# A fused transformer block in one launch: attention transposes within the projections, and two expert tiles ahead of the weight stage

## The chip, the cores and the metric

One core of a Trainium2 chip runs the whole program in one launch. The metric is the time of one execution on the device in microseconds, the median of several; lower is better. Engines in this text: TensorE (PE) multiplies and transposes, VectorE (DVE), ScalarE (ACT) and GpSimd (POOL) work on elements, SyncE (SP) issues the loads and stores.

## The reference, cut to what matters

The input has 256 tokens of width 1024. Two residual layers with a per-layer gated addition come first, then a mixing layer, a cross attention on a memory and a layer of many small experts.

```python
# first attention layer (16 heads of 64), called moba
q, k, v, z = split(rms_norm(x) @ w_in)
q, k = rope(rms_norm(q) * q_gain), rope(rms_norm(k) * k_gain)
x = x + (softmax(q k^T / 8, causal) v * silu(z)) @ w_out
x = x + sigmoid(rms_norm(x) @ w_gate) * (p @ w_proj)
# second layer (nsa): three branches per head (compressed, selected, window), each a
# masked softmax attention, added with learned gates, * silu(z), @ w_out; then the same gated addition
# mixing layer: a linear recurrence beside a chunked attention, @ w_out
# cross attention: 4 heads of 256 on 256 memory rows
x = x + (softmax(q_mem k_mem^T / 16) v_mem) @ w_o_mem
# experts (peer): 8 heads pick 16 of 128*128 experts for each token by two top-16 lists
sc = (h @ w_query) . sub_keys ; top 16 of the sums ; g = softmax(top)
x = x + sum over the picked e of g_e * gelu(h . u_e) * v_e
out = rms_norm(x)
```

## The kernel before

**Projections.** All weight matrices run as one stream of chunks of 512 columns, each in two halves ("units", 1 MB). SP loads a unit into one of four slots. ACT copies it rounded to `whi` (`split`, L1169), POOL writes the rest, weight minus `whi`, into `wlo` (L1093), and PE adds three products, `hThi*whi`, `hThi*wlo`, `hTlo*whi` (`project`, L721), each a pass of 16 matrix products in a half chunk. `whi` and `wlo` hold two units: `split` of a unit waits until PE is done with the unit two before. `take(c)` on ACT (L1188, L1199) first splits two later units and then copies chunk c out of PSUM. For the first layer, chunks 0 to 3 hold q and k, 4 and 5 v, 6 and 7 the gate z. DVE rotates q and k (`rope_chunk`), PE transposes them with the identity (`transposes`, L619) in groups of four blocks into two PSUM banks in turn (a group waits until the one two before is copied), and DVE copies each group out (`take_transposed`, L1573 to L1578). All eight groups of the first layer run between the last projection and the attention.

**Attention.** `attention(phase)` is written out by hand on PE, DVE and ACT as one loop over jobs (a head and a block of 128 queries): PE makes the score of job i (L820), DVE the mask and the maximum (L1744), ACT the exponential (L1270), PE transposes P of job i-3 (L827), ACT copies it out (L1261), PE multiplies by V for job i-4 (L838), DVE scales the result. Scores go to banks 6, 7 and 1 in turn, so they run three jobs ahead; chunks of a projection use banks 0 and 1 or 2 and 3. Phase 0 has 32 jobs, phase 1 96, phase 3 (memory) 8. In phases 0 and 1 `last_gates` puts the tanh of the gate between ACT's jobs (L1246, L1249), and DVE turns it into gate factors. Finished parts of the output are transposed as "pieces" (`piece`, L628), split into `hThi` and `hTlo` by DVE or ACT (L1648, L1207, L1658), and the output projection begins on them (`unit_of_pieces`, L650).

**Experts.** One tile is 128 experts: `u` (1024 columns) and `v` (1024 columns). An activation tile is 24 products (L635, L638) of `u` with the tokens, an output tile 12 products of 512 columns (L1045) in two token halves. While DVE selects the experts, PE computes the activations of the last NA = 30 tiles ahead ("ahead" tiles); E_AT and SEL0_AT say behind which of them exp and the first selection transposes stand. The slots of these tiles end up with `u` and `v` of tiles 0 and 1 (`head`). Then 64 weight groups of four tokens follow: DVE makes one-hot rows (L2101), POOL multiplies the gate in (L1097), PE multiplies the two (L1025), ACT copies the gate weights to `arena` and `kept_w` (L1444, L1445), POOL weighs the ahead tiles (L1103). When these are done SP loads tiles 2, 3, 4, and the tile loop runs: activation of tile i, output of tile i-1; a load waits for the low part of `v` three tiles before. The loop does tiles 0 to 97, the tail the 30 ahead tiles' outputs.

The excerpt that a program prints below shows the functions that the change touches.

Of the kernel before, what the change touches and what calls it, by code (L numbers as in the profile page):

```python
# [8 lines left out]
ALU = mybir.AluOpType  # L9
# [4 lines left out]
P = 128  # L14
# [20 lines left out]
SEL0_AT = 19  # L35
SCALE = HD ** -0.5
# [55 lines left out]
def build(nc, x_d, mem_d, keep_d, tab_d, sml_d, frt_d, final_d, w_d, sk_d, ex_d, out_d):  # L92
    ctx = ExitStack()
    with ctx:
# [116 lines left out]
        half_done, half_out = sem("half_done"), sem("half_out")  # L211
        hot_ready, wt_done, wt_taken = sem("hot_ready"), sem("wt_done"), sem("wt_taken")
# [240 lines left out]
        def piece_of(name, u):  # L453

            src, gain = {"moba_o": (OR, None), "nsa_o": (OR, None), "ple0": (x, "ple_gain0"), "norm1": (x, "norm1"),
                         "ple1": (x, "ple_gain1"), "mem": (OR, "mem"), "cross": (OR, "cross"), "mem_o": (OR, None),
                         "ffn": (OR, "ffn")}[name]
            b = bank[{"moba_o": (0, 0, 0, 4), "nsa_o": (0, 0, 0, 4), "mem_o": (0, 1, 4, 5)}.get(name, (4, 5, 6, 7))[u]]
            return dict(src=src, bank=b, out=b[:, :].rearrange("p (b q) -> p b q", b=2), at=slice(2 * u, 2 * u + 2),
                        gain=None if gain is None else sm(gain)[:, 2 * u:2 * u + 2])  # L460
# [28 lines left out]
        def tr_all(name):  # L489
# [9 lines left out]
                enumerate(sorted(((q // 2, q % 2) for q in range(4)), key=lambda tp: (2 * tp[0] + tp[1] - NA) % 4))]  # L499

# [107 lines left out]
        def _(pe):  # L608
            mm = nc.tensor.matmul

            def transposes(name):
                groups, signals = tr_base(name)
                for i, g in enumerate(TR[NAMES.index(name)][1]):
# [177 lines left out]
            def gated_piece(phase, name, i):  # L791

                if phase == 3:
                    if i == LAST_JOB[3, 1] + 6:
                        pe.wait_ge(o_taken, PHASES[3][LAST_JOB[3, 1]]["number"] + 1)
                        piece(name, 0)
                        piece(name, 1)
                    return
                for u in range(3):
                    if i == piece_ends(phase, u) + 8:  # L800
                        if u > 0:
                            pe.wait_ge(piece_lo[u - 1], nth(name))
# [168 lines left out]
            for u in range(2):  # L971
                pe.wait_ge(piece_lo[u], nth("mem_o"))
# [43 lines left out]
            transposes("sel1")  # L1016
            pe.wait_ge(aa_gelu, NA)
# [116 lines left out]
        def _(act):  # L1134
# [190 lines left out]
            take(first_of("nsa_z") + 1, scale=x_scale)  # L1325
# [106 lines left out]
            for i in range(NA):  # L1432
# [42 lines left out]
            def finish_tile(i, ge, g):  # L1475

                ge(a_done, i + 1)
                ge(glo_ready, i - 1)
                gelu(i)
                ge(v_done, i - 1)  # L1480
# [3 lines left out]
                hi_g(i)  # L1484

            def iteration(i, ge, g):
                if g is not None or i >= 2:
                    loaded(i, ge)
                    ge(a_done, i - 1)
                    hi_u(i)  # L1490
                if i > 0:
                    finish_tile(i - 1, ge, g)
# [5 lines left out]

            expert_loop(act, iteration)
# [22 lines left out]
        def _(dve):  # L1522
# [614 lines left out]
            def iteration(i, ge, g):  # L2137
                if g is not None or i >= 2:
# [3 lines left out]
                if i > 0:  # L2142
# [163 lines left out]
```

## Time and profile before

| | |
|---|---|
| median of 3 runs | 1652.11 us (1650.27 to 1652.24) |
| profiled execution | 1652.1 us, of which span 1650.3 |
| mean granted clock of PE | 0.974 |
| PE busy | 1537.2 us (93%) |
| DVE, ACT, POOL busy | 896.4, 819.6, 567.0 us (54%, 50%, 34%) |
| DMA | 238.47 MB, 145 GB/s on average |

The time of an execution is the span, from the first instruction to the last, and a little around it. A granted clock of 1.00 is PE's upper level, 0.50 its lower. A busy share counts a whole execution; the timeline rows further down show single places.

### The profile page before, as it was taken

What the parts mean: (1) busy time and instruction counts of PE and PEld (TensorE: products, weight loads), DVE (VectorE), ACT (ScalarE), POOL (GpSimd) and SP (SyncE); (2) the same over time, 40 slices, a digit from 0 to 9 for tenths busy, and PEclk for the clock granted to TensorE, in tenths of its full rate; (3) what the DMA queues carried; (4) which work ended last, traced back from release to release, by engine and by line L of the source; (5) the groups of instructions that cost most, each with busy time, mean ns of one, the idle gap of its engine ahead of it and who ended that gap; (6) DMA issues with size and microseconds to landing.
All of it is one profiled execution on the core that took longest, in us unless ns stands there. A gap on an engine that the chain in (4) does not pass through costs nothing.

```text
span 1650.3 us, 28298 instructions
## 1 busy us (share of the span) xinstructions
PE 1537.2 (93%) x10643; PEld 1416.6 (86%) x10643; DVE 896.4 (54%) x2125; ACT 819.6 (50%) x1435; POOL 567.0 (34%) x256
## 2 busy tenths in 40 slices
PE   6998999989979979988999789999999999999998
PEld 5987899978869869978999668999999999999886
DVE  6826248478342332122796894555555555555565
ACT  4546444388434724434455564444444444444444
POOL 5770656510455546725588992000000000000000
PEclk9998999999989979999999999999999999999999
DMA  6750244510233234424254003545555555555453
GB/s 255 274 182 23 106 151 154 206 51 2 78 127 109 97 129 147 159 84 144 81 198 161 1 0 144 188 178 183 195 181 180 189 191 178 182 194 183 172 197 128
DMA packets 37529, 238.47 MB, mean 145 GB/s; under 512 B 4160, under 2 KB 4288, under 8 KB 13248
## 3 DMA queue, kind: packets, MB, share of 16 engines
q1 hardware_dynamic: 37440, 237.27, 40.0%
q8 instruction: 57, 0.93, 0.2%
q14 instruction: 32, 0.26, 0.1%
HBM read 236.21 MB, written 1.05 MB: 144 GB/s over the span
## 4 chain that ended last, share of the span: by engine, by line
PE 65%; POOL 6%; DVE 4%; issue 3%; ACT 3%; POOLq 0%; DVEq 0%; ACTq 0%
PE bank L1045 21%; PE bank L635 15%; PE bank L638 7%; PE bank L718 6%; PE bank L721 4%; POOL raw L1097 3%; PE bank L820 2%; PE bank L678 2%; PE bank L838 2%; POOL wlo L1093 2%; PE bank L650 1%; POOL arena L1103 1%; ACT whi L1169 1%; PE bank L628 1%; PE bank L827 1%
## 5 line engine op out<-in xcount | busy, mean ns | idle before, releaser
L1093 POOL TENSOR_TENSOR wlo<-raw,whi 128x2048 fp32r<-128x2048 f32 x42 | 194.2, 4626 | 204.0 <-ACT whi L1169 204.0
L1093 POOL TENSOR_TENSOR wlo<-arena,whi 128x2048 fp32r<-128x2048 f32 x42 | 193.6, 4615 | 178.2 <-ACT whi L1169 178.2
L635 PE MATMUL bank<-hThi,whi 128*128 128x256 f32 x1024 | 250.3, 282 | 1.2 <-ACT xw L1445 1.2
L635 PE MATMUL bank<-hTlo,whi 128*128 128x256 f32 x1024 | 250.0, 282 | 0.0
L1045 PE MATMUL bank<-whi,ghi 128*128 128x512 f32 x512 | 202.9, 396 | 0.3 <-DVE glo L2133 0.3
L1045 PE MATMUL bank<-whi,glo 128*128 128x512 f32 x512 | 202.9, 396 | 0.0
L1045 PE MATMUL bank<-wlo,ghi 128*128 128x512 f32 x512 | 202.1, 395 | 0.0
L635 PEld LDWEIGHTS bank<-hThi,whi 128*128 128x128 f32 x1024 | 194.7, 190 | 5.6 <-issue 1.6
L635 PEld LDWEIGHTS bank<-hTlo,whi 128*128 128x128 f32 x1024 | 195.0, 190 | 4.2 <-issue 0.2
L1462 ACT ACTIVATE gact<-bank 128x256 f32<-128x256 f32 x98 | 37.8, 386 | 266.6 <-PE bank L638 266.6
L2128 DVE TENSOR_TENSOR gact<-gact,arena 128x256 f32<-128x256 f32 x98 | 41.7, 426 | 201.2 <-ACT gact L1462 201.2
L1169 ACT ACTIVATE whi<-raw 128x2048 fp32r<-128x2048 f32 x42 | 80.5, 1916 | 129.6 <-PE bank L721 60.3
L638 PE MATMUL bank<-hThi,wlo 128*128 128x256 f32 x1024 | 143.7, 283 | 0.0
L1169 ACT ACTIVATE whi<-arena 128x2048 fp32r<-128x2048 f32 x42 | 80.4, 1914 | 120.6 <-PE bank L721 70.3
L638 PEld LDWEIGHTS bank<-hThi,wlo 128*128 128x128 f32 x1024 | 132.1, 192 | 0.0
L2123 DVE TENSOR_TENSOR wlo<-raw,whi 128x1024 fp32r<-128x1024 f32 x84 | 102.9, 1226 | 36.6 <-ACT whi L1466 36.4
L1045 PEld LDWEIGHTS bank<-whi,glo 128*128 128x128 f32 x512 | 96.6, 189 | 23.2
L1045 PEld LDWEIGHTS bank<-whi,ghi 128*128 128x128 f32 x512 | 96.6, 189 | 19.6 <-DVE wlo L2123 0.7
L1045 PEld LDWEIGHTS bank<-wlo,ghi 128*128 128x128 f32 x512 | 96.7, 189 | 19.4
L721 PE MATMUL bank<-whi,hThi 128*128 128x256 f32 x704 | 96.8, 292 | 7.6 <-DVE hThi L1584 7.6
L721 PEld LDWEIGHTS bank<-whi,hThi 128*128 128x128 f32 x704 | 91.5, 200 | 8.4 <-DVE hThi L1584 8.4
L820 PE MATMUL bank<-arena 128*128 128x256 f32 (+1 forms) x320 | 87.5, 369 | 10.0 <-ACT arena L1199 8.0
(287 smaller groups left out, 3167.4 us busy)
## 6 DMA issues: line engine op xcount, KB each, us to landing
raw<-ex_in SPq DMA_DIRECT2D x64, 1024.0 KB, 4.8
raw<-w_in SPq DMA_DIRECT2D x44, 1024.0 KB, 4.8
arena<-w_in SPq DMA_DIRECT2D x44, 1024.0 KB, 4.8
xw<-ex_in SPq DMA_DIRECT2D x32, 1024.0 KB, 4.8
raw<-ex_in SPq DMA_DIRECT2D x54, 512.0 KB, 4.0
xw<-ex_in SPq DMA_DIRECT2D x10, 512.0 KB, 3.8
arena<-frt_in SPq DMA_DIRECT2D x1, 3904.0 KB, 15.2
arena<-tab_in SPq DMA_DIRECT2D x1, 1089.0 KB, 16.2
```

Source lines behind the costliest of these rows:

```text
L635: mm(out, lhs, rhs, start=(k == 0), stop=False)
L638: last = mm(out, lhs, rhs, start=False, stop=(k == len(lo_pairs) - 1))
L718: last = mm(bank[2 * (c % 2) + b][:, T * at:T * at + T], w[:, k, P * j:P * j + P], h[:, k, :], start=first, stop=final)
L721: last = mm(bank[2 * (c % 2) + j][:, UC * half:UC * half + UC], h[:, k, P * j:P * j + P], w[:, k, :], start=first, stop=final)
L820: last = mm(score_bank(phase, i)[:, 0:j["nk"]], j["q"][k], j["k"][k], start=(k == 0), stop=(k == len(j["q"]) - 1))
L1045: last = mm(bank[2 * t + h][:, :], g[:, j % 2, tok], w[:, b, at], start=False, stop=(final and i == 2), skip_group_check=True)
L1093: G.tensor_tensor(wlo[:, u % 2, :], slots[u % RING], whi[:, u % 2, :], ALU.subtract).then_inc(lo_ready, 1)
L1097: G.tensor_tensor(onehot[:, r, 0], onehot[:, r, 0], gate.unsqueeze(2).to_broadcast([P, 4, P]), ALU.mult).then_inc(hotA, 1)
L1169: A(whi[:, u % 2, :], slots[u % RING], ACT.Copy).then_inc(hi_ready, 1)
L1462: A(gact[:, i % 2, :], bank[4 + i % 2][:, 0:T], ACT.Gelu_apprx_tanh).then_inc(a_gelu, 1)
L2123: V.tensor_tensor(wlo[:, b, at], xslots[ex_slot(i)][:, D:2 * D], whi[:, b, at], ALU.subtract).then_inc(vlo_ready, 1)
L2128: V.tensor_tensor(gact[:, i % 2, :], gact[:, i % 2, :], weights, ALU.mult).then_inc(g_ready, 1)
```

## The change

It does four things.

1. PE: the first layer's query and key transposes stand within chunks 6 and 7, two groups at a time. The wait for ACT's last copies (`takenA`), ahead of phases 0 and 1 until now, stands ahead of the third score.
2. ACT, phases 0 and 1: of the two splits ahead of the last `take`, one stays, the other moves into the attention at i = 5; a one-off exponential on two columns stands before the last `take`; the tanh's of phase 0 move from i = 1, 2, 3, 4 to 2, 8, 14, 20.
3. Memory attention: the first two pieces go to banks 6 and 7 instead of 0 and 1, behind a wait for the last mask; the waits for their low parts ahead of the projection go.
4. Experts: the second selection transposes stand behind ahead tile 28 (the 29th); the activations of tiles 0 and 1 are computed from the ahead slots before the weight groups; their outputs run by token halves, the first half behind the last weight group and behind DVE's work on tokens 0 to 127, the second when all weights are there.

```diff
+SEL1_AT = 28
-            b = bank[{..., "mem_o": (0, 1, 4, 5)}.get(name, (4, 5, 6, 7))[u]]
+            b = bank[{..., "mem_o": (6, 7, 4, 5)}.get(name, (4, 5, 6, 7))[u]]
+        head_first = [q for q in head if q[2] == 0]
@@ PE
-            def transposes(name):
+            def transposes(name, some=slice(None)):
                     if i == LAST_JOB[3, 1] + 6:
+                        pe.wait_ge(m_ready, FIRST_JOB[3] + len(PHASES[3]))
             def attention(phase, name=None):
-                if phase < 2:
-                    pe.wait_ge(takenA, taken_before(units_before(name) // 2, "A"))
                 for i in range(len(jobs) + 4):
+                    if phase < 2 and i == 2:
+                        pe.wait_ge(takenA, taken_before(units_before(name) // 2, "A"))
...
-            project_all("moba_in")
+            for c in range(6):
+                project(c)
             pe.wait_ge(roped, 4)
-            transposes("moba_q")
-            transposes("moba_k")
+            transposes("moba_q", slice(0, 2))
+            project(6, lambda: transposes("moba_q", slice(2, 4)))
+            transposes("moba_k", slice(0, 2))
+            project(7, lambda: transposes("moba_k", slice(2, 4)))
             pe.wait_ge(tr_taken, tr_all("moba_k"))
-            pe.wait_ge(takenA, taken_before(first_of("moba_out"), "A"))
             attention(0, "moba_o")
...
-            for u in range(2):
-                pe.wait_ge(piece_lo[u], nth("mem_o"))
...
-            transposes("sel1")
-            pe.wait_ge(aa_gelu, NA)
+                if i == SEL1_AT:
+                    transposes("sel1")
+            for n, (i, tile, part) in enumerate(head_first):
+                pe.wait_ge(auhi_ready, i + 1)
+                pe.wait_ge(aa_gelu, NA - 1 + n)
+                h, l = (w[i % 4].rearrange("p (k n) -> p k n", k=KT) for w in (ahi, alo))
+                products(bank[6 + n % 2][:, 0:T], ...).then_inc(a_done, 1)
+            pe.wait_ge(a_gelu, 2)
...
             def iteration(i, ge, g):
+                if g is None and i < 2:
+                    if i == 0:
+                        for n in range(2):
+                            pe.wait_ge(head_half, n + 1)
+                            out_part(n, 0, False)
+                    ge(glo_ready, i + 1)
+                    out_part(i, 1, False).then_inc(v_done, 1)
+                    return
...
-                if i > 0:
+                if g is not None or i > 2:
-            pe.wait_ge(wt_taken, T // 4 + 8)
@@ ACT
             def last_gates(phase, i):
+                if i == 5:
+                    split()
-                if phase == 0 and i in (1, 2, 3, 4):
-                    at = 256 * (i - 1)
+                if phase == 0 and i in (2, 8, 14, 20):
+                    at = 256 * ((i - 2) // 6)
...
-            for c in range(8):
+            for c in range(7):
                 take(c, scale=x_scale)
+            split()
+            A(sums[:, 8:10], x_scale, ACT.Exp, scale=-1.0)
+            take(7, scale=x_scale, split_first=False)
...
-            take(first_of("nsa_z") + 1, scale=x_scale)
+            split()
+            A(sums[:, 8:10], x_scale, ACT.Exp, scale=-1.0)
+            take(first_of("nsa_z") + 1, scale=x_scale, split_first=False)
...
+            for n, (i, tile, part) in enumerate(head_first):
+                act.wait_ge(a_done, n + 1)
+                A(gact[:, tile, :], bank[6 + n % 2][:, 0:T], ACT.Gelu_apprx_tanh).then_inc(a_gelu, 1)
...
+                if g is None and i < 2:
+                    A(ghi[:, i, P:T], gact[:, i, P:T], ACT.Copy).then_inc(ghi_ready, 1)
@@ DVE, behind the weight groups
+            dve.wait_ge(a_gelu, 2)
+            dve.wait_ge(wt_taken, T // 8 + 8)
+            for n in range(2):
+                last = V.tensor_tensor(gact[:, n, 0:P], gact[:, n, 0:P], Wg[:, T * n:T * n + P], ALU.mult)
+            step(last)
+            for n in range(2):
+                last = V.tensor_copy(ghi[:, n, 0:P], gact[:, n, 0:P])
+            step(last)
+            for n in range(2):
+                V.tensor_tensor(glo[:, n, 0:P], gact[:, n, 0:P], ghi[:, n, 0:P], ALU.subtract).then_inc(head_half, 1)
             dve.wait_ge(wt_taken, T // 4 + 8)
```

DVE multiplies, and takes the low part of, the second token half of both tiles in iterations 0 and 1 in the same way.

## Rows read from the trace of the kernel before

**Rows 1.** The page's first part: busy us, share, instructions.

```profile
PE 1537.2 (93%) x10643; PEld 1416.6 (86%) x10643; DVE 896.4 (54%) x2125; ACT 819.6 (50%) x1435; POOL 567.0 (34%) x256
```

**Rows 2.** Stretches: length, busy us by engine, granted clock, DMA.

```profile
35.10:38.10 3.00, 2.88 (x13) 2.88 (x14) 2.96 (x2) 0.13 (x1) 3.00 (x2) 0.50 0.55 186
...
128.00:134.00 6.00, 5.57 (x18) 4.13 (x18) 2.15 (x10) 5.38 (x20) 0.00 (x0) 0.50 0.00 1
...
1011.30:1640.00 628.70, 628.40 (x3817) 559.63 (x3816) 355.29 (x444) 300.82 (x446) 0.00 (x0) 1.00 0.51 182
```

**Rows 3.** PE timeline: start, length, line, operation, idle before and releaser.

```profile
35.22 3.60 PE L721 MATMUL bank<-wlo,hThi 128*128 128x256 f32 x16 [2.40 <-POOL wlo L1093]
...
560.97 1.46 PE L820 MATMUL bank<-arena 128*128 128x128 f32 x8 [2.16 <-ACT arena L1199]
```

**Rows 4.** PE timeline round the starts of both attentions.

```profile
113.52 2.08 PE L721 MATMUL bank<-whi,hTlo 128*128 128x256 f32 x16
...
124.58 2.10 PE L820 MATMUL bank<-arena 128*128 128x128 f32 x8 [1.91 <-DVE arena L1576]
...
322.11 1.04 PE L619 MATMUL bank<-keep,arena 128*128 128x128 f32 x8
...
322.90 2.15 PE L721 MATMUL bank<-whi,hThi 128*128 128x256 f32 x16
...
332.31 2.05 PE L820 MATMUL bank<-arena 128*128 128x128 f32 x8 [3.31 <-ACT arena L1199]
```

**Rows 5.** DVE timeline of the same places.

```profile
116.08 1.29 DVE L1578 COPY arena<-bank 128x512 f32<-128x512 f32 x2 [31.87 <-PE bank L619]
...
125.53 0.29 DVE L1744 CUSTOM_DVE_ANT_0 arena<-bank,arena 128x128 f32<-128x128 f32 x1 [1.01 <-PE bank L820]
...
329.38 0.34 DVE L1576 TENSOR_SCALAR arena<-bank,arena 128x128 f32<-128x128 f32 x1
```

**Rows 6.** ACT timeline, start of the first attention.

```profile
125.93 1.28 ACT L1270 ACT_TABLE_LOAD   x1 [7.16 <-DVE sc L1744]
...
127.23 0.40 ACT L1270 ACTIVATE arena<-arena,sc 128x128 f32<-128x128 f32 x1
...
127.63 0.61 ACT L1246 ACTIVATE arena<-arena 128x512 f32<-128x512 f32 x1
...
131.99 0.51 ACT L1270 ACTIVATE arena<-arena,sc 128x256 f32<-128x256 f32 x1
```

**Rows 7.** ACT timeline, start of the second attention.

```profile
334.88 0.40 ACT L1270 ACTIVATE arena<-arena,sc 128x128 f32<-128x128 f32 x1
...
338.75 0.51 ACT L1270 ACTIVATE arena<-arena,sc 128x256 f32<-128x256 f32 x1
```

**Rows 8.** PE and DVE timelines round the memory output projection.

```profile
724.42 1.94 PE L650 MATMUL bank<-whi,hThi 128*128 128x256 f32 x8 [3.32 <-DVE hTlo L1658]
...
729.59 2.08 PE L650 MATMUL bank<-wlo,hThi 128*128 128x256 f32 x16
...
721.84 1.28 DVE L1648 CAST hThi<-bank 128x512 fp32r<-128x512 f32 x2
```

**Rows 9.** PE timeline, start and end of the weight groups.

```profile
911.57 5.77 PE L1025 MATMUL bank<-raw 128*128 128x128 f32 x32 [5.58 <-POOL raw L1097]
...
1000.32 1.15 PE L1025 MATMUL bank<-raw 128*128 128x128 f32 x8 [0.24 <-POOL raw L1097]
...
1002.67 0.35 PE L635 MATMUL bank<-hThi,whi 128*128 128x256 f32 x1 [1.20 <-ACT xw L1445]
...
1008.50 0.39 PE L1045 MATMUL bank<-whi,ghi 128*128 128x512 f32 x1
...
1011.30 0.28 PE L635 MATMUL bank<-hThi,whi 128*128 128x256 f32 x1
```

**Rows 10.** ACT and SP timelines: tile 2's load and its split.

```profile
1008.32 1.06 ACT L1459 ACTIVATE whi<-raw 128x1024 fp32r<-128x1024 f32 x1 [1.14 <-DMA raw<-ex_in]
...
1003.13 0.80 SPq L564 DMA_DIRECT2D raw<-ex_in  x2
```

More of the change, by code:

```diff
@@ L211, in build @@
         half_done, half_out = sem("half_done"), sem("half_out")
+        head_half = sem("head_half")
         hot_ready, wt_done, wt_taken = sem("hot_ready"), sem("wt_done"), sem("wt_taken")
@@ L457, in piece_of @@
                          "ffn": (OR, "ffn")}[name]
-            b = bank[{"moba_o": (0, 0, 0, 4), "nsa_o": (0, 0, 0, 4), "mem_o": (0, 1, 4, 5)}.get(name, (4, 5, 6, 7))[u]]
+            b = bank[{"moba_o": (0, 0, 0, 4), "nsa_o": (0, 0, 0, 4), "mem_o": (6, 7, 4, 5)}.get(name, (4, 5, 6, 7))[u]]
             return dict(src=src, bank=b, out=b[:, :].rearrange("p (b q) -> p b q", b=2), at=slice(2 * u, 2 * u + 2),
@@ L609, in _ @@
             mm = nc.tensor.matmul
-            def transposes(name):
+            def transposes(name, some=slice(None)):
                 groups, signals = tr_base(name)
-                for i, g in enumerate(TR[NAMES.index(name)][1]):
+                for i, g in list(enumerate(TR[NAMES.index(name)][1]))[some]:
                     n = groups + i
@@ L1015, in _ @@
                     transposes("sel0")
-            transposes("sel1")
-            pe.wait_ge(aa_gelu, NA)
+                if i == SEL1_AT:
[4 more added lines that the diff above has]
+                h, l = (w[i % 4].rearrange("p (k n) -> p k n", k=KT) for w in (ahi, alo))
+                products(bank[6 + n % 2][:, 0:T], [(h[:, k, :], t[:, k, :]) for k in range(KT) for t in (hThi, hTlo)],
+                         [(l[:, k, :], hThi[:, k, :]) for k in range(KT)],
+                         lambda: pe.wait_ge(aulo_ready, i + 1)).then_inc(a_done, 1)
+            pe.wait_ge(a_gelu, 2)
             pe.wait_ge(tr_taken, tr_all("sel1"))
@@ L1475, in finish_tile @@
             def finish_tile(i, ge, g):
[L1477 to L1480, printed above, removed]
+                if g is not None or i >= 2:
+                    ge(a_done, i + 1)
+                    ge(glo_ready, i - 1)
+                    gelu(i)
+                    ge(v_done, i - 1)
                 if g is not None or i >= 2:
@@ L1483, in finish_tile @@
                 ge(g_ready, i + 1)
-                hi_g(i)
+                if g is None and i < 2:
+                    A(ghi[:, i, P:T], gact[:, i, P:T], ACT.Copy).then_inc(ghi_ready, 1)
+                else:
+                    hi_g(i)
             def iteration(i, ge, g):
[L1487 to L1491, printed above, removed]
+                if g is None and i < 2:
+                    finish_tile(i, ge, g)
+                    return
+                loaded(i, ge)
+                ge(a_done, i - 1)
+                hi_u(i)
+                if g is not None or i > 2:
                     finish_tile(i - 1, ge, g)
@@ L1497, in tail_hi @@
                     hi_v(i)
+            act.wait_ge(a_done, 2)
             expert_loop(act, iteration)
@@ L2137, in iteration @@
             def iteration(i, ge, g):
+                if g is None and i < 2:
+                    if i == 0:
+                        for n in range(2):
+                            V.tensor_tensor(gact[:, n, P:T], gact[:, n, P:T], Wg[:, T * n + P:T * n + T],
+                                            ALU.mult).then_inc(g_ready, 1)
+                    ge(ghi_ready, i + 1)
+                    V.tensor_tensor(glo[:, i, P:T], gact[:, i, P:T], ghi[:, i, P:T], ALU.subtract).then_inc(glo_ready, 1)
+                    return
                 if g is not None or i >= 2:
@@ L2141, in iteration @@
                                     ALU.subtract).then_inc(ulo_ready, 1)
-                if i > 0:
+                if g is not None or i > 2:
                     finish_tile(i - 1, ge, Wg[:, T * (i - 1):T * i] if g is None
                                 else rounds[:, i - 2, bass.ds(g, 1)].rearrange("p g t -> p (g t)"), g)
+            dve.wait_ge(a_gelu, 2)
[6 more added lines that the diff above has]
+            step(last)
+            for n in range(2):
+                V.tensor_tensor(glo[:, n, 0:P], gact[:, n, 0:P], ghi[:, n, 0:P], ALU.subtract).then_inc(head_half, 1)
             dve.wait_ge(wt_taken, T // 4 + 8)
```

## The prediction

> **What bounds the kernel now.** I read the page's busy shares first, then busy time and granted clock by stretch, then each engine's timeline round the places that the change touches. TensorE (PE) is busy 93% of the span [rows 1]. From 1011.30 to 1640.00 us, the expert tile loop and its tail, it is idle for 0.30 us of 628.70 at full clock [rows 2]: nothing there waits for ScalarE (ACT), VectorE (DVE) or a load, so time saved ahead of it reaches the end whole. What can be saved are PE's holes at the stage boundaries, and what follows them: the clock. After an idle stretch of 2.40 us PE got 0.50, the lower level of 1.2 GHz, for 3 us; after one of 2.16 us it kept 1.00, 2.4 GHz [rows 2, 3]. In the first attention it still had 0.50 from 128 to 134 us [rows 2]. The change works at four such holes. The sum is made against the profiled execution, 1652.1 us, of which 1650.3 are span and 1.8 lie around it; it equals the median of the runs, 1652.11.
>
> **1. First attention's start: -5.4 us.** The last three passes of 16 products start at 113.52 and issue for 1.92 us, so the projection ends at 115.44; the first score starts at 124.58 [rows 4]. Between them stand eight groups of four transposes, each pair of groups waiting for DVE's copies out of PSUM. Moved between half chunks they wait for nothing: a pair has a whole half chunk (three passes, 5.8 us) for its copies, and the fourth rotated chunk, for which PE waits, is done 30 us before (DVE's idle time ahead of its first copy is 31.87 us [rows 5]). They still cost PE time: eight transposes inside a projection took 322.90 - 322.11 = 0.79 us [rows 4], so 32 cost 3.2 us and the projection ends at 118.6.
> The first two scores now start there; only the third waits for ACT's last copies. Before, the mask started 0.95 us after the scores, at 125.53 [rows 5]; add 0.4 for it, and its result is there at 120.0. ACT had first split weights (1.9 us) and copied only then. Now it has the function table loaded beforehand, copies the last chunk at once (two copies 0.6 us apart), and is free by 120.1. The first exponential moves from 127.23 [rows 6] to about 120.1: -7.1. Of this 1.28 us is the table load, which stood on the path after the first mask (125.93 [rows 6]).
> By the Trainium skill, "ScalarE: Activation LUTs", What ACT_TABLE_LOAD costs, a switch of set is a load of about 1.28 us plus a drain of about 1.38 us. The load agrees with [rows 6]; of a drain the row shows nothing, the exponential follows 1.30 us after the load's start. With the page's sum each of the two preloads would bring 1.4 us more.
> Given back: one weight split (1.9 us) is put into ACT's queue ahead of the sixth job, and three of four gate tanh's, which ran in the first four jobs, move to jobs 8, 14 and 20. From the first to the sixth exponential it was 131.99 - 127.23 = 4.8 us with four tanh's; in the second attention, same shapes, 3.9 us with one short tanh [rows 6, 7]. I take 3.6 for the jobs, 0.5 for one tanh (0.61 at 127.63 [rows 6], less its overlap with the next) and 1.8 for the split: 5.9. The sixth exponential comes at 126.0 instead of 131.99, -6.0. What is queued behind the split: exponentials, then PE's transposes of P, then the products with V; scores and masks run at most three jobs ahead. After it, three tanh's at 0 to 0.5 us each, taken as 0.4 since ACT is busy 5.4 of 6 us in the row from 128 [rows 2]: +1.2. PE at full clock there instead of 0.50 from 128 to 134 [rows 2]: -0.6. Sum -5.4; ends -3.2 (everything added counts whole, clock falls again) and -7.5 (the split hides in ACT's waits).
>
> **2. Second attention's start: -2.4 us.** No transposes move. PE waited 3.31 us for ACT's split and copy before its first score at 332.31 [rows 4]. Now the score waits only for DVE's last transposed keys, done at 329.38 + 0.25 [rows 5]: it starts at 329.7. With 0.95 and 0.3 for the mask and no table load, the first exponential comes at 331.0 instead of 334.88 [rows 7], -3.9. First to sixth then takes 3.6 + 1.8 = 5.4 instead of 3.9: 336.4 instead of 338.75 [rows 7], -2.4. Ends -1.2 and -3.8.
> For both: the split that comes later is of weights used after the attention, and POOL's half of it and the next load have the attention's length for cover.
>
> **3. Memory output projection: -3.7 us.** The pieces 0 and 1 move from the projection's output banks to banks 6 and 7, free once the last mask has read its scores; the added wait for that mask holds nothing, since the pieces come after it anyway. So PE need not wait for DVE's low parts (3.32 us idle, first product at 724.42), only for the high parts, the first of which starts at 721.84 and takes 0.6 [rows 8]. Chain: 722.6 first pair of products (0.5), 723.2 second, 723.7 two pieces (8 transposes, 0.9), ACT's and DVE's high parts to 725.3, two pairs to 725.9, then the low pass. That pass started at 729.59 [rows 8]: -3.7. It needs the clock to stay up, as idle falls from 3.32 to 1.4 us; if it falls all the same, -2.0. Ends -1.9 and -4.2.
>
> **4. Selection and expert tiles 0, 1: -3.1 us.** At the front PE idles 5.58 us before the first weight group at 911.57 [rows 9], waiting for POOL's last low part, then DVE, then POOL. The two activation tiles (5.83 us, 1002.67 to 1008.50 [rows 9]) go there. DVE's first one-hot rows come 0.4 us later (the selection's transposes now stand ahead of tile 29, whose end releases POOL's last part), and PE waits for the second gelu: the first group starts at about 912.3, +0.7, but at full clock (8 products took 1.15 us at 1000.32 [rows 9], about twice that at half clock). So ACT and POOL, which sets the pace, are about 0.3 us ahead after it: -0.3.
> At the back the last group issues until 1001.45. DVE has tokens 0 to 127 ready by then: six instructions on 128x128, 0.3 us each, after its last one-hot rows. PE runs both tiles' outputs as halves, no longer waiting 1.20 us [rows 9]: two outputs of 2.80 us (1008.50 to 1011.30 [rows 9]), to 1007.1. Tile 2's load was issued at 1003.13 and is not moved; ACT split it at 1008.32 [rows 10], so PE starts tile 2 at 1009.4 instead of 1011.30. This is a new wait of 2.3 us. Two activations (5.8) and 0.3 for ACT's and DVE's chain, which no longer has an output as cover, and output 2 starts at 1015.5. Before, tile 2's activation at 1011.30 was followed by output 1 and activation 3, 8.5 us in all, and output 2 came at 1019.8: -4.3. The 2.3 us lies between 2.16 (clock kept) and 2.40 (fell) [rows 3]; it is nearer the second, so I take a fall: 3 us at half clock as in the row from 35.10 [rows 2], +1.5. Sum -0.3 - 4.3 + 1.5 = -3.1. Ends -1 (fall, late front) and -4.9.
>
> Together -5.4 - 2.4 - 3.7 - 3.1 = -14.6: 1637.5 us. The dropped waits that are not named were met already; they cost and bring nothing.
>
> **Rivals.** A: the clock stays up in the gap before tile 2. For it: 2.16 us was survived; against: 2.40 was not. 1637.5 - 1.5 = 1636.0.
> B: the split empties the attention pipelines, which then run at the pace of their waits: all that is put in counts whole and the clock falls in the hole. For it: PE, DVE and ACT hand each job on, three ahead at most; against: masks and scores for three jobs stand ready when the split ends. 2.2 + 1.2 us less: 1640.9.
> C, slower: the tile loop loses cover. Tile 5's load is issued when tile 2's second low part is done, about 2 us earlier than before, while PE wants tile 5 about 4.3 earlier. If loads then arrive late in every round, 96 looped tiles each pay. From 0.15 us per tile (14.6/96) the whole gain is gone; at 0.25 the time is 1661.5. Against it: PE idles 0.30 us in 628.70 [rows 2], and load, split and low part together (5.2 from issue to split [rows 10], then 1.1 and 1.2) are shorter than the 9 us that stay.
> D, no change: the attentions' ends are set by DVE's gating chain and the new wait for tile 2 eats the rest, 1652. Nothing in the timeline supports it.
>
> **How the numbers follow.** Forecast 0.50, A 0.22, B 0.23, C 0.03, D 0.02. The time is the forecast's, 1637.5. The range takes in A and B and the ends of the terms without letting all fall on one side (all together would be 1644.8 and 1631.7): 1633.0 to 1643.0. Measurement of this kernel tells 0.2%, 3.3 us, from no change; faster by more has 0.95 (forecast, A, B), within it 0.02, slower 0.03.
>
> **What would show it.** Right: no transposes between the last projection pass and the first score, first exponential within 2 us of that pass's end; table loads ahead of the last copy in both input stages; PE idle before the second attention under 1.2 us; clock 1.00 in both starts; the memory projection's first products 1.4 us after PE stops; weight groups preceded by two activation tiles; a PE gap of about 2.3 us before tile 2. Wrong: clock 0.50 after the sixth job in either attention (B), PE idle again within the tile loop (C), the first weight group more than 1 us late against POOL's previous start, or hole lengths as before.

## The result and the profile after

| | before | after |
|---|---|---|
| median | 1651.57 us (4 runs) | 1634.46 us (4 runs, 1632.88 to 1635.24) |
| profiled execution, its span | 1652.1, 1650.3 us | 1634.4, 1632.6 us |
| mean granted clock | 0.974 | 0.984 |

The ratio is 0.9894, 95% interval 0.9882 to 0.9907: 1.1% faster. Predicted were 1637.5 us and 1633.0 to 1643.0. Lines of the kernel after are 4 to 37 higher than those of the rows of before.

The page's first part, as [rows 1]: PE's busy time falls by 9.5 us of the 17.7, with as many instructions (10643) as before; the mean granted clock is 0.984 instead of 0.974.

```profile
PE 1527.7 (94%) x10643; PEld 1407.4 (86%) x10643; DVE 903.1 (55%) x2131; ACT 818.9 (50%) x1437; POOL 566.8 (35%) x256
```

Stretches, as [rows 2]: the first attention's start and the tile loop. Granted clock is the third column from the right. The first attention starts at 1.00 now; the tile loop has no holes still.

```profile
126.00:134.00 8.00, 7.42 (x55) 6.69 (x56) 4.51 (x20) 7.30 (x29) 4.09 (x1) 1.00 0.35 125
...
1001.28:1622.00 620.72, 619.87 (x3754) 551.50 (x3755) 350.76 (x439) 297.03 (x440) 0.00 (x0) 1.00 0.52 183
```

PE's timeline at the edited places, as [rows 4, 8, 9]. In order: the last transposes and pass of the first projection, the first two scores, the third score; the second attention's first score; the memory output projection's first products and low pass; the first and the last weight group; the first output half, tile 2's activation, output 2.

```profile
112.22 1.03 PE L623 MATMUL bank<-keep,arena 128*128 128x128 f32 x8
...
116.92 2.08 PE L725 MATMUL bank<-whi,hTlo 128*128 128x256 f32 x16
118.84 0.61 PE L825 MATMUL bank<-arena 128*128 128x128 f32 x4
120.36 0.71 PE L825 MATMUL bank<-arena 128*128 128x128 f32 x4 [0.91 <-ACT arena L1219]
...
321.94 1.47 PE L825 MATMUL bank<-arena 128*128 128x128 f32 x8 [0.78 <-DVE arena L1613]
...
712.37 1.25 PE L654 MATMUL bank<-whi,hThi 128*128 128x256 f32 x8 [1.57 <-DVE hThi L1685]
...
716.01 2.08 PE L654 MATMUL bank<-wlo,hThi 128*128 128x256 f32 x16
...
898.64 1.60 PE L1038 MATMUL bank<-raw 128*128 128x128 f32 x12 [0.47 <-ACT gact L1468]
...
986.08 1.15 PE L1038 MATMUL bank<-raw 128*128 128x128 f32 x8 [0.24 <-POOL raw L1117]
987.73 0.47 PE L1058 MATMUL bank<-whi,ghi 128*128 128x512 f32 x1 [0.50 <-DVE glo L2200]
...
995.04 0.39 PE L639 MATMUL bank<-hThi,whi 128*128 128x256 f32 x1 [1.46 <-ACT whi L1489]
...
1001.28 0.47 PE L1058 MATMUL bank<-whi,ghi 128*128 128x512 f32 x1 [0.23 <-DVE glo L2170]
```

ACT's timeline, as [rows 6, 7]: the table load early, then last copies, first exponential, the moved split, the sixth exponential.

```profile
114.42 1.28 ACT L1309 ACT_TABLE_LOAD   x1
...
119.05 1.26 ACT L1219 ACTIVATE arena<-bank,sc 128x512 f32<-128x512 f32 x2 [3.13 <-PE bank L725]
120.34 0.40 ACT L1292 ACTIVATE arena<-arena,sc 128x128 f32<-128x128 f32 x1
...
123.58 1.90 ACT L1189 ACTIVATE whi<-raw 128x2048 fp32r<-128x2048 f32 x1
125.39 0.50 ACT L1292 ACTIVATE arena<-arena,sc 128x256 f32<-128x256 f32 x1
```

DVE's and POOL's timelines at the two places that the prediction did not see. One is a clamp (the sum of a row held above a small bound) of 3 columns in the second attention, 0.16 us elsewhere, beside POOL's low part of the moved split. The other is the head tiles' two products behind the weight groups (3.48 and 0.28 us, the pair 3.68).

```profile
328.31 4.09 DVE L1769 TENSOR_SCALAR sc<-sc 128x3 f32<-128x3 f32 x1 [0.88 <-ACT arena L1292]
...
983.01 3.68 DVE L2194 TENSOR_TENSOR gact<-gact,arena 128x128 f32<-128x128 f32 x2
```

```profile
327.86 4.51 POOL L1113 TENSOR_TENSOR wlo<-arena,whi 128x2048 fp32r<-128x2048 f32 x1 [6.73 <-ACT whi L1189]
```

Where the 17.7 us of the profiled pair came from, by how much earlier each milestone comes (steady: the same distance for every later job):

| step | milestone | change, own share | predicted |
|---|---|---|---|
| 1 | steady exponentials of the first attention | -7.85 | -5.4 |
| 2 | the same of the second attention | -0.97 | -2.4 |
| | up to the last exponential of the memory attention (715.63 to 705.27) | -1.5 | 0 |
| 3 | low pass of the memory output (729.59 to 716.01) | -3.2 | -3.7 |
| 4 | last weight group (1000.32 to 986.08) | -0.7 | -0.3 |
| 4 | output 2 (1019.83 to 1001.28) | -4.3 | -4.3, +1.5 clock |
| | end | +0.85 | 0 |

### The profile page after: what moved, and what is told of

The parts are those of the page before. It is cut to its first block, busy times and chain, and to the rows that moved or that the text cites. A ratio compares the mean times of both kernels' runs of the same rounds, so it can differ in the third digit from the quotient of the medians.

```text
span 1632.6 us, 28309 instructions
## 1 busy us (share of the span) xinstructions
PE 1527.7 (94%) x10643; PEld 1407.4 (86%) x10643; DVE 903.1 (55%) x2131; ACT 818.9 (50%) x1437; POOL 566.8 (35%) x256
## 4 chain that ended last, share of the span: by engine, by line
PE 64%; POOL 6%; DVE 4%; ACT 3%; issue 3%; DMA 1%; POOLq 0%; DVEq 0%; ACTq 0%; SPq 0%
PE bank L1058 21%; PE bank L639 15%; PE bank L642 7%; PE bank L722 6%; PE bank L725 4%; POOL raw L1117 3%; PE bank L825 2%; PE bank L682 2%; PE bank L843 2%; POOL wlo L1113 2%; PE bank L654 1%; POOL arena L1123 1%; ACT whi L1189 1%; PE bank L632 1%; PE bank L832 1%
## 5 line engine op out<-in xcount | busy, mean ns | idle before, releaser
L725 PE MATMUL bank<-wlo,hThi 128*128 128x256 f32 x704 | 93.7, 287 | 2.4 <-POOL wlo L1113 2.4
```

The costliest lines, as they stand in the source:

```text
L725: last = mm(bank[2 * (c % 2) + j][:, UC * half:UC * half + UC], h[:, k, P * j:P * j + P], w[:, k, :], start=first, stop=final)
```

## The experiments

Unless said otherwise each edit is made to the changed kernel, and each is profiled once. "Lead" is how much earlier than in the profile of before something comes; "own" is without what was led or lost ahead of the stage. Every lead is taken against the one profile of before. In 7 of 14 profiles (before, after, e2, e4, e5, e9, e10) PE's clock is 0.50 for some 3 us at about 36 us, in the others not, and these are 1.0 to 1.5 us ahead from there on; "own" leads of the first attention leave that out, taking it from ScalarE's splits between 60 and 100 us.

**e1: the clamp in PSUM.** For the second attention's first 16 jobs:

```diff
-issue(V.tensor_scalar(factor, total, 1e-30, None, ALU.max))
+issue(V.tensor_scalar(scratch, total, 1e-30, None, ALU.max))   # bank[0]
-issue(V.reciprocal(factor, factor))
+issue(V.reciprocal(scratch, scratch))
-issue(V.tensor_tensor(factor, factor, gates, ALU.mult))
+issue(V.tensor_tensor(factor, scratch, gates, ALU.mult))
```

> In the second attention's first 16 jobs the clamped sum, its reciprocal and the input of the product with the gates stand in PSUM (bank 0, free there) instead of SBUF; nothing else of the changed kernel is touched. Theory (VectorE's 4.09 us clamp at 328.31 waited for GpSimd's 4.51 us low part, because both were working on SBUF alone): the clamp takes about 0.2 us again, the exponential of job 8 comes at about 331 instead of 333.5, and the steady lead of the second attention grows by 2.0 to 2.7 us: span about 1630.2. Rival (the ScalarE split of 1.9 us at the sixth job empties the pipeline, and the long clamp is only idle time seen in another form): the clamp may look short, but the masks around it still come late and the steady lead grows by under 0.5 us.

Measured 1632.84 us (1630.35 to 1633.96), ratio to before 0.9888 [0.9874, 0.9902]. DVE's timeline, the same clamp beside a low part of 4.52 us on POOL from 326.72:

```profile
327.16 0.17 DVE L1769 TENSOR_SCALAR bank<-sc 128x3 f32<-128x3 f32 x1 [0.88 <-ACT arena L1292]
```

The clamp is short, and at job 8 the attention's own lead is 2.9 us, not 0.7: the rival falls. Half of the theory's gain did not arrive: from about 328 to 335 us the clock was 0.50, and the steady own lead is 0.39. Whether that counts against the edit, e4 shows. The edit moves the reciprocal and one input of the product too; the clamp is the one of the three that had been long.

**e2: POOL's low part in quarters.**

```diff
-G.tensor_tensor(wlo[:, u % 2, :], slots[u % RING], whi[:, u % 2, :], ALU.subtract).then_inc(lo_ready, 1)
+# for this one unit: four instructions of 512 columns, the last with then_inc
```

> GpSimd's low part that runs in the second attention's start (4.51 us in the changed kernel) is made by four instructions of 512 columns, about 1.15 us each, instead of one of 2048. If VectorE's blocked clamp gets SBUF between two GpSimd instructions, it takes at most 1.2 us instead of 4.09, and about 2 us of the loss at job 8 go. If it must wait until GpSimd falls idle, as the 3.68 us of the first-half products behind GpSimd's stream at 983.01 suggest, it stays at 3.5 to 4.1 us and nothing is gained.

Measured 1635.63 us, one execution. DVE's and POOL's timelines:

```profile
328.84 0.84 DVE L1772 TENSOR_SCALAR sc<-sc 128x3 f32<-128x3 f32 x1 [0.88 <-ACT arena L1295]
```

```profile
328.39 4.94 POOL L1115 TENSOR_TENSOR wlo<-arena,whi 128x512 fp32r<-128x512 f32 x4 [6.73 <-ACT whi L1192]
```

The clamp ends at 329.68, where POOL's first quarter ends (328.39 + 4.94/4 = 329.6). It waits for one instruction, not for POOL to be idle. At job 8 the attention's own lead is 2.7 us, the 2 us more that the first case forecast; with a slow stretch behind it the steady own lead is 0.38. The Trainium skill, "SBUF — State Buffer", Who interferes with whom, has this as a lock: VectorE's two-port forms of `tensor_scalar`, and its instructions with two SBUF inputs when GpSimd's reads SBUF, contend with GpSimd for one port pair, which is held for a whole instruction. Both runs agree with it.

**e3: both splits ahead again.**

```diff
-                if i == 5:
-                    split()
             split()
+            split()
             A(sums[:, 8:10], x_scale, ACT.Exp, scale=-1.0)    # in both input stages
```

> Both weight splits stand ahead of the last copy again in both attentions (as before the change); the early table load, the spread tanh's and all of TensorE's changes stay. Theory: in the first attention the moved split was free, so the first exponential and the steady part come 1.9 us later (steady lead -5.9 instead of -7.85). In the second attention the first exponential also comes 1.9 us later, but GpSimd's low part is over before VectorE's first clamp, so the jump of 2.7 us at job 8 is gone and the steady part is 0.8 us earlier than in the changed kernel. Together +1.1 us: span about 1633.7. Rival (a split inside the attention costs its 1.9 us in either place): first attention +0, second +0 to -0.8, span 1631.8 to 1632.6.

Measured 1635.85 us (1634.03 to 1642.35), ratio 0.9915 [0.9899, 0.9932]; profiled span 1639.5. The first exponential came 3.4 us later (own lead 3.47 instead of 6.84), not 1.9. ACT's timeline shows why:

```profile
117.95 1.91 ACT L1189 ACTIVATE whi<-raw 128x2048 fp32r<-128x2048 f32 x1 [4.71 <-PE bank L725]
119.88 1.28 ACT L1308 ACT_TABLE_LOAD   x1
```

The second split waits for PE, and the table load stood behind it, so it was early no more: 1.9 + 1.3. Both theories missed that. No clamp was long, and the second attention's own lead was 0.1. The moved split is what makes the early load possible. Two of the six executions, the profiled one among them, took 1641.25 and 1642.35 us, the other four 1634.03 to 1636.60. In the profiled one 2.3 us of the difference to the profile after lie between the second attention and the end of the memory attention, in code that no kernel here changes; why is open.

**e4: tile 2's load without the wait for POOL.**

```diff
             sp_.wait_ge(wt_done, T // 4)
-            sp_.wait_ge(wm_taken, T // 4)
             for i in range(2, 2 + XRING):
+                if i == 4:
+                    sp_.wait_ge(wm_taken, T // 4)
```

> The loads of expert tiles 2 and 3 wait only for TensorE's last weight group, since their slots hold nothing but one-hot rows; only tile 4's load, whose slot holds the kept weights, still waits for GpSimd's last product. Theory (the load of tile 2 sets the 1.46 us gap on TensorE ahead of tile 2): it is issued at about 987.3 instead of 989.03, the gap is 0 to 0.2, and the time falls by 1.3 to 1.5 us, span about 1631.2. Rival (ScalarE's or VectorE's work on the second halves sets it, or transfers share their bandwidth and land no earlier): gap over 1 us, time within 0.5 us of the changed kernel.

Measured 1632.32 us (1628.52 to 1634.82), ratio 0.9882 [0.9868, 0.9897]. The last weight group started at 987.92, output 2 at 1001.39: 13.47 us instead of 15.20, with no gap ahead of tile 2. The load did set that gap. But the profiled span is 1632.9, 0.3 above the changed kernel's: up to the expert stage this kernel is the changed kernel, and yet it reached the last group 1.84 us later. Two rows of stretches show where, from the second attention's start, the changed kernel's first and then e4's:

```profile
330.00:334.00 4.00, 1.85 (x13) 1.45 (x12) 3.97 (x12) 1.51 (x8) 2.37 (x1) 1.00 0.16 33
```

```profile
330.00:334.00 4.00, 3.35 (x14) 2.65 (x14) 3.97 (x11) 1.51 (x9) 2.54 (x1) 0.50 0.15 20
```

Same code, same hole of 1.52 us and same clamp of 4.09; in one execution the clock fell behind it (to 340 us), in the other not. The second attention's own lead, in the five profiles with the code of the changed kernel up to there: 0.97 (after, e5), -0.19 and -0.21 (e6, e11), -1.51 (e4); mean 0. With the clamp in PSUM: 0.39 (e1) and 1.74 (e9).

**e5: the head halves in PSUM, tiles 2 and 3 loaded when their slots are free.**

```diff
+step(V.tensor_copy(bank[4][:, 2 * P:4 * P]..., gact[:, :, 0:P]))   # head_act(n): its half n
-V.tensor_tensor(gact[:, n, 0:P], gact[:, n, 0:P], Wg[...], ALU.mult)
+V.tensor_tensor(head_act(n), head_act(n), Wg[...], ALU.mult)       # high and low part likewise
+sp_.wait_ge(wt_done, T // 4 - 2 * (3 - i))                         # i = 2, 3; for 4 wm_taken
```

> Two edits of the changed kernel. VectorE first copies tokens 0 to 127 of both head tiles to PSUM (bank 4, free by then), and product, high and low part read them there, so that none of the four steps has more than one input in SBUF. The load of tile 2 waits only for weight group 62, after which nothing reads its slot, the load of tile 3 for group 64. Theory (the two products took 3.68 us at 983.01 because SBUF was held by GpSimd's stream): each step takes 0.3 to 0.4 us, the low parts are done before TensorE's last group, TensorE goes from that group into the first output half with under 0.1 us idle instead of 0.50, and tile 2 follows without a gap. From the last weight group (986.08 in the changed kernel) to output 2 (1001.28) it was 15.20 us; it becomes 13.3 (less 0.45 and 1.46). Rival (VectorE simply reaches this point late, or the product waits for data of the last groups): the products still take over 3 us or start later, TensorE keeps the 0.50, and the stretch is 13.7 to 13.8.

Measured 1631.80 us (1628.75 to 1633.34), ratio 0.9880 [0.9865, 0.9896]; span 1630.4. DVE's timeline:

```profile
982.99 0.42 DVE L2198 COPY bank<-gact 128x256 f32<-128x256 f32 x1
983.44 0.50 DVE L2200 TENSOR_TENSOR bank<-bank,arena 128x128 f32<-128x128 f32 x2
```

0.50 us for the pair instead of 3.68, and no hole on PE from the last group (986.05) to output 2 (998.78): 12.73 us, 0.6 better than expected. Its slow stretches up to the expert stage happened to be those of the profile after, so the spans compare: 2.2 us less.

**e6: the loads 0.8 us later.**

```diff
             sp_.wait_ge(wm_taken, T // 4)
+            sp_.wait_ge(glo_ready, 2)
```

> The loads of tiles 2, 3 and 4 wait also for VectorE's second low part of the second halves (989.1 + 0.69 in the changed kernel), so they are issued 0.8 us later and TensorE's gap ahead of tile 2 grows from 1.46 to about 2.3 us, the size that the prediction gave it. By the prediction's fourth step the clock falls to 0.50 for about 3 us behind it: from the last weight group to output 2 it takes 15.20 + 0.8 + 1.5 = 17.5 us. By rival A the clock stays at 1.00: 16.0 us.

Measured 1635.36 us, one execution. PE's timeline and the stretches around it:

```profile
994.93 0.39 PE L640 MATMUL bank<-hThi,whi 128*128 128x256 f32 x1 [2.20 <-ACT whi L1490]
```

```profile
986.00:995.00 9.00, 6.30 (x29) 4.70 (x27) 2.30 (x9) 2.71 (x6) 0.99 (x2) 1.00 0.53 207
995.00:1000.00 5.00, 5.00 (x29) 5.00 (x30) 2.36 (x2) 1.45 (x3) 0.00 (x0) 0.66 0.61 257
```

A gap of 2.20 us, and the clock fell behind it: 17.45 us from the last group (985.23) to output 2 (1002.68). With the gap that the forecast assumed, its 1.5 us of slow clock do come, in this execution; rival A would have given 16.0.

**e7 and e8: one engine's part of the attention starts alone, on the kernel before.**

```diff
# e7, PE
+            project(6, lambda: transposes("moba_q", slice(2, 4)))     # and the other groups
+                    if phase < 2 and i == 2:
+                        pe.wait_ge(takenA, ...)
# e8, ACT
+                if i == 5:
+                    split()
+            A(sums[:, 8:10], x_scale, ACT.Exp, scale=-1.0)
+                if phase == 0 and i in (2, 8, 14, 20):
```

> The kernel before with only TensorE's part of the attention starts: the transposes within chunks 6 and 7, and the wait for ScalarE's last copies ahead of the third score. Of the parts of the two attention starts alone: the projection ends 3.2 us later (118.6), ScalarE's split and copies follow it to 122.0 and the table load to 123.3, so the first exponential comes 3.9 us earlier than before (127.23) and not 7: ScalarE takes over as the bound. In the second attention the first exponential comes 1.3 to 1.5 us earlier (ScalarE's copies end at 332.05, then the load). Steady lead over before: -3.9 and -5.3; time about 1646. Rival (the two halves of the change are independent, and TensorE's part brings most): first exponential -5 us or more, time 1644 or less.

> The kernel before with only ScalarE's part of the attention starts: one of two splits moved into the sixth job, the early table load, the spread tanh's. First attention: ScalarE was idle 7.16 us ahead of the table load, so only the load's 1.28 us go, and the moved split costs its 1.9 less what the tanh's gave: steady lead 0 to -1.0. Second attention: first score 1.9 us and first exponential 3.2 us earlier, but VectorE's clamp waits behind GpSimd's low part (about 4 us) as in the changed kernel: steady lead of this attention 0 to -1.0 with TensorE's clock up, +1 to +2.5 if it falls there. Sum 0 +- 2, time about 1651. Rival (all added work hides in waits): steady leads -1.3 and -3.2, time about 1647.

Measured e7 1647.29 us (11 runs), ratio 0.9974 [0.9965, 0.9983]; e8 1649.49 (12 runs), 0.9991 [0.9983, 1.0]. Own leads: e7 3.70 at the first exponential and 3.60 steady (expected 3.9), then 0.75 in the second attention (expected 1.4); e8 1.29 and 1.41 (expected 1.28, and 0 to 1.0 steady), then -0.84 (expected -1 to -2.5 for this case) with the clock down behind the clamp, which took 4.09 us here too. ACT's timelines, e7 first:

```profile
119.81 1.25 ACT L1201 ACTIVATE arena<-bank,sc 128x512 f32<-128x512 f32 x2
121.07 1.28 ACT L1272 ACT_TABLE_LOAD   x1
122.36 0.40 ACT L1272 ACTIVATE arena<-arena,sc 128x128 f32<-128x128 f32 x1
```

```profile
124.98 0.40 ACT L1272 ACTIVATE arena<-arena,sc 128x128 f32<-128x128 f32 x1 [9.03 <-DVE sc L1751]
```

In e7 ACT goes from copies through the load to the exponential without a pause, it is the bound; in e8 it idles 9.03 us. 3.60 and 1.41 make 5.0, the two together 7.8: neither engine could use the other's time.

**e9: both repairs**, the edits of e1 and e5.

> The changed kernel with the two repairs that the earlier runs support: VectorE's clamp and reciprocal of the second attention's first 16 jobs read and write PSUM, the head tiles' first halves are worked on in PSUM, and the loads of tiles 2 and 3 go out as soon as their slots are free. Theory: the gains add, since the stages follow each other: 2.4 us at the expert stage (12.73 instead of 15.20 from the last weight group to output 2), and 1.9 us in the second attention (its own lead at job 8 2.9 us instead of 0.7, of which a slow stretch of TensorE's clock takes about 2.5 back as it did with this edit alone, where the same stretch costs the changed kernel as much). Median about 1630.3; range 1628.5 to 1632. Rival (the lead won in the second attention is lost to the clock every time): about 1631.8, as with the expert edits alone.

Measured 1631.93 us (1629.52 to 1633.53), ratio 0.9879 [0.9862, 0.9895]; profiled span 1627.7. Both mechanisms are there (clamp 0.17; 12.74 us from the last group to output 2), but the median is that of the rival. The intervals of e1, e4, e5, e9 and the changed kernel overlap: none is shown to be faster than it by its time, e9 least doubtful with 2.5 us of medians.

**e10: without the early table loads**, both one-off exponentials taken out.

> The changed kernel without the two early exponentials that load ScalarE's table. By the rows the load of 1.28 us then stands behind the last copies (which end at 120.3 and 322.3 in the changed kernel): the first exponential of the first attention comes 1.3 us later, that of the second 0.7 us later (there the mask is ready only 0.6 after the copies), and the steady leads shrink by the same. By the Trainium skill's page "ScalarE: Activation LUTs", What ACT_TABLE_LOAD costs, a drain of about 1.38 us comes with a load: 2.7 and 2.0 us later.

One execution, 1639.08 us. ACT's timeline in both attentions:

```profile
119.20 1.27 ACT L1219 ACTIVATE arena<-bank,sc 128x512 f32<-128x512 f32 x2 [4.64 <-PE bank L725]
120.48 1.28 ACT L1292 ACT_TABLE_LOAD   x1
121.78 0.40 ACT L1292 ACTIVATE arena<-arena,sc 128x128 f32<-128x128 f32 x1
...
324.36 1.28 ACT L1292 ACT_TABLE_LOAD   x1 [0.58 <-issue]
325.65 0.40 ACT L1292 ACTIVATE arena<-arena,sc 128x128 f32<-128x128 f32 x1
```

First attention 1.28 us later and steady 1.27 less: the load and nothing for a drain, as the rows of before had it. Second: 1.27 us later, not 0.7. The load did not begin when the copies ended at 323.78 but 0.58 later, with the mask: it belongs to the exponential and waits with it. The steady part missed by more: the second attention's own lead was -1.4 at job 8 (0.7 in the changed kernel) and -3.6 steady, with slow stretches of the clock between 325 and 330 us and between 336 and 343.

**e11: the waits for the low parts back.**

```diff
+            for u in range(2):
+                pe.wait_ge(piece_lo[u], nth("mem_o"))
             c = first_of("mem_o")
```

> The changed kernel with TensorE's waits for the low parts of the first two pieces back ahead of the memory output projection; the pieces stay in banks 6 and 7. Theory (the wait, not the banks by themselves, cost the time): TensorE waits for VectorE's second low part, 1.27 + 0.7 us longer, so its idle ahead of the first products is 3.3 us again instead of 1.57, and from the last exponential (705.27 in the changed kernel) to the low pass (716.01), 10.74 us, becomes 12.5 at full clock and up to 14 if the clock falls. Rival (VectorE's high parts of the later pieces set the low pass anyway): 11.0 or less.

One execution, 1635.64 us. PE's timeline:

```profile
714.01 1.19 PE L654 MATMUL bank<-whi,hThi 128*128 128x256 f32 x8 [3.32 <-DVE hTlo L1697]
...
717.60 2.08 PE L654 MATMUL bank<-wlo,hThi 128*128 128x256 f32 x16
```

The wait of 3.32 us is back to the hundredth; from the last exponential (705.16) to the low pass 12.44 us instead of 10.74, at full clock (1.00 from 705 to 725). In the kernel before it was 13.96 with the clock at 0.50 from 724.5 to 728. So of the 3.2 us, 1.7 is the wait; the other 1.5 goes with the slow stretch, which neither e11 nor the changed kernel has.

**e12: the tanh's early again**, `i in (1, 2, 3, 4)` instead of (2, 8, 14, 20).

> The changed kernel with the four gate tanh's of the first attention in jobs 1 to 4 again, ahead of the moved split. By the prediction's first step: three more tanh's ahead of the sixth exponential, 0.5 us each, so that one comes 1.5 us later, and the steady lead loses 1.5 less the 1.2 that the later tanh's were to cost: 0.3. If instead the three later tanh's stand in ScalarE's waits and cost nothing, as the steady lead of 7.85 against 6.6 at the sixth job suggests, the steady lead loses 1.0 to 1.5 us (6.4 to 6.9 instead of 7.85), more if TensorE's clock falls in the hole.

One execution, 1635.01 us. First exponential as in the changed kernel (own lead 6.83), sixth 5.19 instead of 6.56, steady 5.06 instead of 7.81: 2.75 us lost, of which 1.37 by the sixth job and the rest behind it, where a slow stretch returned:

```profile
126.00:131.00 5.00, 4.67 (x27) 4.67 (x28) 1.32 (x8) 3.35 (x16) 4.23 (x1) 0.66 0.02 3
```

## Why the prediction was right, and where not

The forecast of 1637.5 was 3.0 us too high, inside its range. That it is so near is partly luck, for its misses have both signs: steps 1 and 4 and the code between brought 5.9 us more than forecast, steps 2 and 3 and the end 2.8 less.

**Step 1, -5.4, measured -7.85.** The mechanism held: two scores right behind the last pass, exponential at 120.34 (predicted 120.1). (The pass at 113.52 [rows 4] is the last of three, not all three; the end that the prediction takes from it is right.) The term mis-sized is what was given back. The sixth exponential came at 125.39 (predicted 126.0), and the three later tanh's, +1.2 in the sum, cost nothing: the exponential at i = 20, where one stands, has a lead of 7.52, the one before 7.85 and the one behind 7.86. I read "busy 5.4 of 6 us" of a stretch [rows 2] as no room; but that stretch held three of the early tanh's. Where the later ones go ACT had room, 4.94 us busy of 6 before and 5.37 after (the fourth busy time of a row):

```profile
134.00:140.00 6.00, 6.00 (x48) 5.58 (x47) 3.66 (x17) 4.94 (x19) 0.00 (x0) 1.00 0.01 3
```

```profile
134.00:140.00 6.00, 6.00 (x49) 5.52 (x47) 4.82 (x21) 5.37 (x22) 0.00 (x0) 1.00 0.03 11
```

The lead grew behind the sixth job, from 6.60 to 7.85, by 1.25 where the sum has 0.6 for the clock; no run separates what the clock gave there. In e12 the tanh's in their old places cost 2.75 us, 1.37 of it by the sixth exponential and the rest where the clock fell. All eight profiles with these starts (after, e1, e2, e4, e5, e6, e9, e11) have a steady own lead of 7.8.

**Step 2, -2.4, measured -0.97 in the profiled pair and 0 on average.** First exponential -4.1 (predicted -3.9). The step that failed is its last sentence, that POOL's half of the split has the attention's length for cover. Nobody waited for the result of POOL's work, but DVE's clamp waited 4.09 us while it ran, and with the clamp the mask of job 8, ACT (idle 2.5 us) and PE (idle 2.15). e1 removes it and e2 shortens it. Rival B named the right symptom, waits at the pace of a drained pipeline, with another cause; the fall of the clock that it forecast came in three of the five profiles (e4, e6, e11).

The profile of before had shown such a wait, in a place that the change does not touch. DVE's and POOL's timelines there: 2 columns take 4.57 us and end with POOL's low part.

```profile
20.62 4.57 DVE L1535 TENSOR_SCALAR sc<-sc 128x2 f32<-128x2 f32 x1
```

```profile
20.11 5.06 POOL L1093 TENSOR_TENSOR wlo<-raw,whi 128x2048 fp32r<-128x2048 f32 x1
```

In the first attention the same low part (at 125.56 in the profile after) held nothing up. Its jobs have no clamp; their reciprocal, from SBUF to SBUF too, took 0.17 us beside it:

```profile
128.24 0.17 DVE L1767 RECIPROCAL sc<-sc 128x4 f32<-128x4 f32 x1
```

**Step 3, -3.7, measured -3.2.** Right, and e11 splits it; the first products came 1.57 us after PE stopped, not 1.4, and the chain behind took 0.3 more.

**Step 4, -3.1, measured -5.0.** -4.3 at output 2 as worked out; the front gave 0.66 instead of 0.3. The clock did not fall, so rival A held, but for a reason that neither named: the gap was 1.46 us, not 2.3. PE reached it later (of this 0.50 us behind DVE's products, which e5 takes out) and the issue-to-split time was shorter, 4.90 us instead of 5.19 [rows 10]. DVE's six instructions, priced at 0.3 us each and done before the last group ends, took 4.8 us (983.01 to 987.78). Where the gap was 2.20 (e6), the clock fell. No run takes this part of the change alone: the -4.3 rests on the rows, and e4, e5 and e6 vary what stands around it.

**Not in the sum.** +0.85 behind output 2, of it 0.54 at the tail's first low part (PE's wait at 1546.52), and -1.5 between the attentions, where slow stretches behind the same holes fell differently. From the second attention's last exponential to the memory attention's last, code that no kernel here changes took 297.2 to 301.0 us: the profiled pair's 300.2 and 298.6 are two draws from that. What decides between them stays open.

**Rivals C and D.** PE idles 0.85 us in 620.72 of the tile loop and tail; no load is late. C and D are out.

## What to carry to other kernels

Work moved into a pipelined stage is to be priced by what it occupies, not only by who waits for its result: a 4.5 us GpSimd subtraction held up a 3-column VectorE clamp, and putting the clamp's output in PSUM undid that. Look in the profile of before for small instructions that take long, and for what runs beside them. A hole worth closing has two sides (here TensorE's transposes and ScalarE's split and table load), and the two edits gave 3.6 and 1.4 us alone and 7.8 together. Holes whose lengths are the same can cost the clock in one execution and not in the next, so judge a 1 us edit by its own stage in the trace, and by several traces.

## What the runs showed of the hardware

- A VectorE `tensor_scalar` from SBUF to SBUF waited until the GpSimd instruction beside it ended: it took 4.09 us beside one of 4.51, 0.84 beside a first quarter, and 0.17 with its output in PSUM (e1). Not every VectorE instruction on SBUF waits: a reciprocal took 0.17 us beside one of 4.53 (128.24). A product with two SBUF inputs (983.01, e5's counterpart 0.50) waited 3.48 us although GpSimd's instructions there took only 1.04 and 0.44 each, until that stream paused; why it did not get in between two of them is open.
- The length of a hole does not decide alone whether TensorE's clock falls: behind 2.16 us it kept 1.00 in the profile before and fell in e6's (552 to 556 us); near 35 us it fell after 1.97 us (e4) and stayed up after 2.46 (e1). What the prediction read from two rows, 2.16 kept and 2.40 fell, is therefore no rule. The Trainium skill, "TensorE: Matmul & The Clock Gate", Part 1, says that the chip's activity sampling runs free of the kernel's start, which would make it chance; the same code falling and not falling agrees with that.
- A ScalarE table load that comes with an exponential begins only when the exponential's own waits are met (e10), and takes 1.28 us with no drain behind it.
